# The first microseconds of an attention and SwiGLU block in another order: norm weights spread by matmuls with a row of ones, token tiles and weight units loaded in turn

## The reference

```
y = x32 * rsqrt(mean(x32 * x32, axis=-1) + EPS)
h = y * g                     # g: 2048 norm weights, the same for every token
proj = h @ w_in               # w_in: 2048 x 5168; q, k, v, compressed k and v, gates
```

## Time and profile before

| | us |
|---|---|
| median of 3 runs | 2363.2 (2360.5 to 2365.2) |
| the profiled execution: its own time | 2363.04 |
| its span in the profile | 2361.3 |
| PE busy | 2306.7 (98%) |
| DVE busy | 1323.8 (56%) |
| ACT busy | 776.3 (33%) |

### The profile page before, as it was taken

One profiled execution on the slowest core, in us unless ns is written; L12 is line 12 of the kernel. 1 busy time (PEld: TensorE's weight loads), 2 busy tenths in 40 slices (PEclk: granted clock), 3 DMA queues, 4 the chain that ended last, 5 costly groups with the idle time before them and its releaser, 6 DMA issues.

```text
span 2361.3 us, 32149 instructions
## 1 busy us (share of the span) xinstructions
PE 2306.7 (98%) x12083; PEld 1971.6 (83%) x12083; DVE 1323.8 (56%) x1984; ACT 776.3 (33%) x1147; POOL 75.9 (3%) x88
## 2 busy tenths in 40 slices
PE   7999999999999999999999999999999999999998
PEld 6898888888889989888888888888888888888886
DVE  5333565666666556446464655656564646464657
ACT  4332344443443334323232322323232233222322
POOL 1000000000000000000000000000000000000000
PEclk9999999999999999999999999999999999999999
DMA  5343211212114222245345354545353525354444
GB/s 173 117 115 91 63 55 55 63 54 55 54 61 145 64 63 72 89 135 152 116 126 142 102 149 116 143 114 137 107 143 100 150 90 152 107 143 125 118 115 134
DMA packets 225615, 254.09 MB, mean 108 GB/s; under 512 B 14187, under 2 KB 188288, under 8 KB 224176
## 3 DMA queue, kind: packets, MB, share of 16 engines
q1 hardware_dynamic: 218192, 223.40, 31.1%
q0 software_dynamic: 7264, 28.51, 6.3%
HBM read 224.59 MB, written 4.19 MB: 97 GB/s over the span
## 4 chain that ended last, share of the span: by engine, by line
PE 93%; DVE 5%; ACT 1%; issue 1%; DMA 1%; SPq 0%; DVEq 0%; ACTq 0%; POOL 0%
PE ps L1211 90%; PE ps L1505 1%; DVE wl L725 1%; DVE x_rows L1144 1%; DMA x_rows<-in_x_dram 0%; PE ps L1255 0%; PE ps L1497 0%; DVE nmax L990 0%; PE ps L1541 0%; DVE ptl L1010 0%; DVE ffn_work L1166 0%; DVE ffn_work L1169 0%; ACT ptc L439 0%; ACT sq L442 0%; DVE pbuf L1004 0%
## 5 line engine op out<-in xcount | busy, mean ns | idle before, releaser
L1211 PE MATMUL ps<-hTh,wh 128*128 128x512 f32 (+1 forms) x1968 | 769.3, 391 | 9.1 <-DVE ql L725 3.2
L1211 PE MATMUL ps<-hTh,wl 128*128 128x512 f32 (+1 forms) x1968 | 761.2, 387 | 0.0
L1211 PE MATMUL ps<-hTl,wh 128*128 128x512 f32 (+1 forms) x1968 | 760.4, 386 | 0.0
L725 DVE TENSOR_TENSOR wl<-raw,wh 128x1024 fp32r<-128x1024 f32 x298 | 363.1, 1222 | 347.4 <-ACT wh L439 346.3
L439 ACT ACTIVATE wh<-raw 128x1024 fp32r<-128x1024 f32 x298 | 314.5, 1059 | 553.1 <-PE ps L1211 447.2
L1211 PEld LDWEIGHTS ps<-hTh,wh 128*128 128x128 f32 x1968 | 371.4, 189 | 86.4 <-issue 5.8
L1211 PEld LDWEIGHTS ps<-hTh,wl 128*128 128x128 f32 x1968 | 370.7, 188 | 75.4
L1211 PEld LDWEIGHTS ps<-hTl,wh 128*128 128x128 f32 x1968 | 371.2, 189 | 71.7 <-issue 0.2
L725 DVE TENSOR_TENSOR wl<-down,wh 128x1024 fp32r<-128x1024 f32 x132 | 161.4, 1223 | 157.3 <-ACT wh L439 157.2
L1211 PE MATMUL ps<-wh,opsh 128*128 128x512 f32 x616 | 240.6, 391 | 6.0 <-DVE opsl L725 3.8
L1211 PE MATMUL ps<-wl,opsh 128*128 128x512 f32 x616 | 240.2, 390 | 0.0
(11 more groups left out here) (175 smaller groups left out, 2063.0 us busy)
## 6 DMA issues: line engine op xcount, KB each, us to landing
raw<-in_ffn_w_gate_dram SPq DMA_DIRECT2D x176, 256.0 KB, 3.1
raw<-in_ffn_w_up_dram SPq DMA_DIRECT2D x176, 256.0 KB, 3.0
down<-in_ffn_w_down_dram SPq DMA_DIRECT2D x176, 256.0 KB, 3.3
raw<-in_nsa_w_in_dram SPq DMA_DIRECT2D x164, 256.0 KB, 3.0
raw<-in_nsa_w_out_dram SPq DMA_DIRECT2D x64, 256.0 KB, 3.2
t<-in_ffn_w_down_dram SPq DMA_DIRECT2D x44, 256.0 KB, 3.3
down<-down POOLq DMA_DIRECT2D x22, 512.0 KB, 6.0
t<-down POOLq DMA_DIRECT2D x22, 512.0 KB, 6.2
```

The lines of the kernel that those rows point to most:

```text
L725: nc.vector.tensor_tensor(dst, src, hi.bitcast(f32), ALU.subtract).then_inc(done, 1)
L1211: return nc.tensor.matmul(out_, a, b, start=start, stop=stop, skip_group_check=True)
```

## The change

The broadcasting DMA is gone. A DMA of one row (8 KB) loads the norm weights to `gain_line` in one partition; POOL sets a row of 128 ones; PE multiplies ones by the line in four unsplit float32 matmuls of 512 columns, into PSUM banks 4 to 7; DVE copies the four banks to `gain_row`. The loads are issued in the order gain line, x tile 0, x tile 1, unit 0, x tile 2, unit 1, x tile 3, then unit 2 on. ACT, DVE and PE take the steps in another order, and PE waits for single banks of `hT_lo` where it waited for whole tiles.

```
+        ones, gain_line = over("ones", [1, P], q_at + 20 * 1024), over("gain_line", [1, D], q_at + 24 * 1024)
...
-            for t in range(TT):
+            def x_tile(t):
                 sp.dma_start(x_rows[:, t, :], x[0, t * P:(t + 1) * P, :]).then_inc(x_loaded[t], 16)
-                if t == 0:
-                    sp.dma_start(gain_row[:, :], mix_g.to_broadcast([P, D])).then_inc(gain_loaded, 16)
+
+            sp.dma_start(gain_line[:, :], mix_g).then_inc(gain_loaded, 16)
+            x_tile(0)
+            x_tile(1)
...
                         unit(n, k_halves(n, w_in_v[q][:, :, c:c + 256], 4))
+                        if n < 2:
+                            x_tile(2 + n)
...
+            pool.memset(ones[:, :], 1.0).then_inc(ones_ready, 1)
...
             hidden_columns(0)
+            split(0)
             hidden_columns(1)
-            split(0)
             sum_squares(2)
             split(1)
             sum_squares(3)
+            split(2)
             hidden_columns(2)
-            split(2)
...
-                    dve.wait_ge(gain_loaded, 16)
+                    dve.wait_ge(gain_ready, 4)
...
+            for c in range(4):
+                dve.wait_ge(gain_banks, c + 1)
+                nc.vector.tensor_copy(gain_row[:, c * 512:(c + 1) * 512], bank(4 + c)).then_inc(gain_ready, 1)
             norm(0)
             norm(1)
             hidden_columns(0)
-            hidden_columns(1)
+            hidden_columns(1, [0])
             split(0)
+            hidden_columns(1, [1])
+            split(1)
+            hidden_columns(1, [2, 3])
             norm(2)
-            split(1)
+            split(2)
             norm(3)
             hidden_columns(2)
-            split(2)
             hidden_columns(3)
             split(3)
...
+            pe.wait_ge(ones_ready, 1)
+            pe.wait_ge(gain_loaded, 16)
+            for c in range(4):
+                mm(bank(4 + c), ones[:, :], gain_line[:, c * 512:(c + 1) * 512], True, True).then_inc(gain_banks, 1)
+            pe.wait_ge(consts_ready, 1)
             hidden_columns(0)
+            pe.wait_ge(gain_ready, 4)
             hidden_columns(1)
+            for n in range(2):
+                pe.wait_ge(hT_lo, 5 + n)
+                first_unit(n, 0)
+            hidden_columns(2)
             pe.wait_ge(hT_lo, 8)
-            first_unit(0, 0)
-            hidden_columns(2)
-            first_unit(1, 0)
+            first_unit(2, 0)
             hidden_columns(3)
-            first_unit(2, 0)
+            for n in range(3):
+                pe.wait_ge(hT_lo, 13 + n)
+                first_unit(n, 1)
             pe.wait_ge(hT_lo, 16)
-            for n in range(3):
-                first_unit(n, 1)
```

More of the change, by code:

```diff
@@ L165, in nsa_swiglu_block @@
         vector_done = sem("vector_done")
+        ones_ready, gain_banks, gain_ready = sem("ones_ready"), sem("gain_banks"), sem("gain_ready")
         ss_done, rms_den, rms_root, h_ready = sem("ss_done"), sem("rms_den"), sem("rms_root"), sem("h_ready")
@@ L742, in norm, with hidden_columns @@
                                                in1=gain_row[:, :], op0=ALU.mult, op1=ALU.mult).then_inc(h_ready, 1)
-            def hidden_columns(t):
-                for q in range(4):
+            def hidden_columns(t, qs=range(4)):
+                for q in qs:
                     dve.wait_ge(hT_hi, 4 * t + q + 1)
@@ L1242, in tokens_half @@
                     last.then_inc(units_used, 1)
-            pe.wait_ge(consts_ready, 1)
             def hidden_columns(t):
```

## The result

After takes **2373.3 us** (median of 5 runs, 2370.0 to 2376.3) against 2363.2 (5 runs, 2360.5 to 2365.2). The ratio is 1.0040, 95% interval 1.0029 to 1.0051: 10 us **slower**, where I had said 3.5 faster. The profiled execution took 2373.29, span 2371.2.

The account below looks back on a forecast made before the run. PE, busy 98% of the span, was taken as the bound. Its unit 0 half 1 would start 2.9 us earlier, 3.7 if the clock rose in the transposes; 3.5 taken off gave 2359.7 us, range 2356.5 to 2363.3.

Parts of the forecast that it names:

- its first part: Whole run: one long PE queue, PE busy 98% of the span, so start gains reach the end if PE stays fed.
- My last sentence: Conditions for being wrong: first PE row after 5 us, eight instructions before 7.5, no norm 2 wait, new waits after 40.
- rival B: Gain matmuls at the start cost one cycle a column, gain ready at 7.6 us; total 2358.4 us, chance 0.10.
- the load arithmetic: Loads at the start: without 1 MB of writes ahead, at 401 GB/s, tile 1 lands at 8.9 us instead of 13.04.
- the forecast 2.9: Start of unit 0 half 1 on PE: 36.7 us against 39.57, 2.9 us earlier.
- the rise: PE's clock going to full speed 5.5 us into the transposes starting at 13.4, making the gain 3.7 us.
- the rule that the prediction had set beside it: Trainium skill, PE clock: transposes do not count as busy as matmuls do; by it the gain stays 2.9 us.
- C: The gain line lands 5.7 us after issue, leaving 0 to 0.4 us of gain; total 2363.0 us, chance 0.12.
- A: PE's clock rises in the gain matmuls and stays up until the transposes; 5.0 us gained, 2358.2 us, chance 0.20.
- D: Thinner PE work keeps early units and transposes at half clock; unit 0 half 1 at 43.8, total 2370 us, chance 0.06.
- the yardstick: Start of unit 0 half 1 on PE, 39.57 us originally; PE's remaining work from there was taken as unchanged.

Follow-up runs that it names:

- a_mid4: Changed kernel plus 16 idle PE instructions (4 tiny products) between the attention and feed-forward loops: 2363.9 us, ratio 0.9995.
- a_pad16: Changed kernel plus 64 idle PE instructions (16 tiny products) at the start, ahead of both loops: 2361.3 us, ratio 0.9982.
- better: Changed kernel with tile 0's norm in two halves, splits of units 0 and 1 moved earlier, and 16 tiny products at the start: 2359.4 us, ratio 0.9979.
- better_nopad: The kernel better without its 16 tiny products: 2370.7 us, ratio 1.0031.
- b_mid5: Original kernel plus 20 idle PE instructions (5 tiny products) between the attention and feed-forward loops: 2373.0 us, ratio 1.0036.
- b_pad69: Original kernel plus 276 idle PE instructions (69 tiny products) in PE's first wait: 2373.2 us, ratio 1.0034.
- b_pad15: Original kernel plus 60 idle PE instructions (15 tiny products) ahead of the first transposes: 2372.7 us, ratio 1.0027.
- a_pad4: Changed kernel plus 16 idle PE instructions (4 tiny products) at the start, ahead of both loops: 2366.5 us, ratio 1.0008.
- loads_only: Original kernel with gain line, its matmuls and copies, and new load order, but old step order; 17 tiny products added: 2360.9 us, ratio 0.9984.
- steps_only: Changed kernel with the old broadcasting DMA and old load order, keeping the new step order; 20 tiny products added: 2363.3 us, ratio 0.9995.

## Why the prediction was wrong

**The step that failed** is in its first part: "what PE has left from there is the same before and after", and with it "a microsecond won or lost at the start moves the end by about as much". The instructions that PE has left are the same; the time they take is not. Three jumps took 9.4 us more by the lag. In medians, undoing them gave 9.4 (a_mid4 under after), 12.0 (a_pad16 under after) and 11.3 us (better under better_nopad), and causing them alone cost 8.4 (b_mid5 over before); the medians of before, by batch, lie 2 us apart, so the first two are good to about that. I had counted the added instructions by their time only and not by the place they push later code to; no rival had it. My last sentence named the sign ("if PE has new waits after 40 us"), without a price.

**What is shown and what is argued.** Shown: the loss follows the number of PE instructions ahead of the loop and not the schedule (b_mid5, a_mid4), it comes back after 256 (b_pad69), and it sits behind backward jumps. The traces tie it to code as well, by three things worked out from their records:

- Each of the 15 gaps behind feed-forward jumps and the 4 behind attention jumps (two each in b_pad15 and a_pad4) ends 1.24 to 1.58 us after the end of a 16,384-byte code transfer that began behind the jump; in a_pad16 such a transfer runs from 1304.21 to 1305.09 at the same place, and PE goes on through it.
- From the end of the attention jump to the gap PE's queue has 32 rows in a_pad4 and 12 in b_pad15, at both jumps: 20 fewer, and b_pad15 has 59 - 39 = 20 more ahead. So the gap stands at one place of the code, and adding instructions ahead moves the jump's target towards it.
- That place gives the length: a_pad4 has nine matmuls more to run meanwhile, and its gaps are 1.53 and 1.37 us where those of b_pad15 are 2.50 and 2.77.

Argued, as no row shows a code address: that this place is the end of a block, and that PE uses up the rest behind the jump's target before the next block is there. The feed-forward loop fits less sharply: with 19, 20 or 275 rows over before PE starts 3 to 5 matmuls between jump and gap and with 23 only 1 to 3. The Trainium skill (Runtime: NRT & Kernel Launch, "Instruction fetch mechanics") says that code is fetched in blocks of 256 instructions, in sequence only, and that a taken branch to a block that is not held must wait for a fetch. The trace agrees on the block (16,384 bytes) and b_pad69 on the 256; the price is measured here.

**The start, term by term.** The gain line stands in the chain of waits of after:

```profile
0.74 1.70 DMA gain_line<-in_norm_mix_g_dram
```

It landed at 2.44 (forecast 3.1: what I took as 2.35 us was 1.70). The eight instructions took 7.16, the forecast 7.0 at half clock and two cycles a column, so rival B (one cycle) is out. Norm 0 multiplied at 11.31 (11.0), norm 1 at 14.40 (14.1), transposes at 13.81 (13.4), unit 0 at 21.52 (20.9), unit 1's split at 23.85 (24.0) behind ACT's squares, norm 2 at 27.00 (27.1). The squares of tile 1 stand in the timeline of ACT after:

```profile
8.99 1.91 ACT L463 ACTIVATE x_sq<-x_rows 128x2048 f32<-128x2048 f32 x1 [0.98 <-DMA x_rows<-in_x_dram]
```

8.99 where the load arithmetic had 8.9. 3.0 us of the forecast 2.9 arrived, and that close a match is partly luck:

- The forecast let norm 0 multiply as soon as the gain was ready, at 11.0, and left out the 0.83 from mean to multiplication that it used for norm 1, though the mean stands behind the copies on DVE. In after the last copy ended at 10.46 and the multiplication began 0.85 later. The gain line, which landed 0.66 early, hid most of it.
- The forecast's 2.9 held for a clock that does not rise in the transposes; with the rise it had 3.7. The clock did rise there (6.41 us for 32, where 0.219 each at half clock make 7.15), against the rule that the prediction had set beside it. But ACT, which had copied unit 0 first, was through the last bank only at 20.84, and unit 1's split began at 23.85, as forecast without a rise.

**The other rivals.** C is out with the landing at 2.44. A is out: the gain matmuls took as long as half clock makes them, and 32 transposes took 6.41 us, not the 3.8 of twice 1.91. D is out: unit 0 ran at full clock at once, its starts 0.12 apart from 21.8. D alone had the sign (2370, measured 2373.3), but on the wrong ground: it looked for a half clock in the first 45 us.

**Still open** is the smaller loss. With starts alike, the lag at about 900 us was -0.4 (after), +0.1 (a_pad16) and +0.4 us (a_mid4), so the 3 us are gone, while at 40 us all three were 3 ahead. It goes in clock drops of 3.4 us, each worth 1.4 to 1.5: after has them at 258, 562, 736 and 835, before at 413 and 884, and both one of 10.2 at 706. Two more drops are 2.9 us, which is about the loss.

Where they fall is not mere chance: a_pad16 and a_mid4 have those at 736 and 835 too, and b_mid5 has those of before (412 and 883). But their number is not fixed for a kernel. The granted clock of before's executions in batch 3 lies between 0.992 and 0.996, and one drop of 3.4 us takes 0.0007 off it (an estimate: 1.7 of 2361 us), so they differ by five or so drops, and one profile of each kernel does not settle a difference of two. The medians do not settle it either: they put a_pad16 4.0 us under the before of its batch, a_mid4 only 0.6, loads_only 3.4 and steps_only 1.0, with 3.0, 3.0, 2.0 and 1.3 won at the yardstick. The profiled executions of a_pad16 and a_mid4 were the slowest of their runs (2364.5 and 2366.2).

Nor did I map which counts are clear of both loops: 0 and 85 to 87 over before are; 19, 20, 23 and 275 hit the feed-forward loop, 59 the attention loop, 39 the attention loop slightly. a_mid4 is clear with 23 ahead of the attention loop and 39 ahead of the other.

## What to carry to other kernels

Where a long engine queue holds loops, an edit ahead of them can cost or win a few microseconds at every backward jump (here about 2 to 4), whatever it does itself: compare the waits with the releaser "issue" behind each jump in both traces before explaining a difference at the place of the edit, and repeat the edit with a few dozen idle instructions more. Then choose the count that is clear of all loops; here that was worth 9 to 12 us, three to four times what the reordered start brought at the yardstick. A start that only feeds the bound engine earlier passes its gain on to the end only as far as nothing behind takes it back.

## What the runs showed of the hardware

- A backward jump of the feed-forward loop costs PE 0 to 0.3 us when no gap follows (at 1304 in before two starts are 0.30 and 0.33 apart instead of 0.227; at 1303.7 in a_pad16 none is). In PE's queue the taken branch itself stands 3.3 to 3.9 us in every kernel, with or without gaps, and the last branch of a loop, which is not taken, 0.08: most of a taken branch is hidden, as PE still has matmuls to run. At unlucky places 2.2 to 3.2 us passed from start to start (1.4 and 1.5 in a_pad4), often followed by 3.4 us at 1.2 GHz, another 1.6 us. b_mid5 had a gap of 2.24 and no drop behind it (0.33 to 0.23 between starts from 1306.79), so the gap alone does not decide it.
- The clock rose *during* transposes. In after the clock record begins, at full, at 19.4 us, amid 32 transposes that followed 4.07 us of idling, and unit 0 began at full speed at 21.52. In before two bursts of transposes of 3.7 us had not raised it.
- Loading one row of 8 KB took 1.70 us from issue to landing on SP's queue with nothing ahead of it; POOL's loads of 0.5 to 32 KB took 5.7 to 7.2 us at the same time.
